# Two of VectorE's and TensorE's steps of an S5 scan given to GpSimd, in a fused decoder block

## What is computed

```python
lam_bar = jnp.exp(lam * dt)                       # complex, per state
b_bar = ((lam_bar - 1.0) / lam)[..., None] * bmat
bu = jnp.einsum("gpc,blgc->blgp", b_bar, ug.astype(jnp.complex64))
_, states = lax.associative_scan(_lin_rec, (a_el, bu), axis=1)   # s_t = lam_bar * s_(t-1) + bu_t
y = jnp.einsum("gcp,blgp->blgc", cmat, states).real + d_skip * ug
...
h = h + merged @ w_out[i]
```

## Time and profile before

| | |
|---|---|
| median of 3 runs | 1686.86 us (1686.63 to 1687.17) |
| the profiled execution, its time | 1687.59 us |
| its span from first to last instruction | 1686.0 us |
| granted TensorE clock, share of full speed | 0.998 |
| busy: PE, DVE, ACT, POOL | 1673.8, 1321.9, 971.6, 177.0 us |
| share of the span | 99%, 78%, 58%, 10% |
| DMA, mean | 209 GB/s |

### The profile page before, as it was taken

One profiled execution on the slowest core, in us unless ns is written; L12 is line 12 of the kernel. 1 busy time (PEld: TensorE's weight loads), 2 busy tenths in 40 slices (PEclk: granted clock), 3 DMA queues, 4 the chain that ended last, 5 costly groups with the idle time before them and its releaser, 6 DMA issues.

```text
span 1686.0 us, 24685 instructions
## 1 busy us (share of the span) xinstructions
PE 1673.8 (99%) x8468; PEld 1399.1 (83%) x8468; DVE 1321.9 (78%) x1677; ACT 971.6 (58%) x1271; POOL 177.0 (10%) x262
## 2 busy tenths in 40 slices
PE   9999999999999999999999999999999999999997
PEld 8888888888888888888878888888888888888886
DVE  7999999999998987545765868888888888845555
ACT  7776777667666667434547755444444444454553
POOL 7834201110000000000000200000000000000001
PEclk9999999999999999999999999999999999999999
DMA  7655555554566566666786577777777777756653
GB/s 254 213 185 175 185 173 179 169 181 163 196 218 219 190 220 187 201 197 195 243 266 208 170 231 243 241 241 244 243 243 242 236 245 236 234 190 198 190 188 123
DMA packets 167656, 352.19 MB, mean 209 GB/s; under 512 B 16112, under 2 KB 32672, under 8 KB 167456
## 3 DMA queue, kind: packets, MB, share of 16 engines
q1 hardware_dynamic: 162528, 338.26, 61.9%
q0 software_dynamic: 4336, 12.07, 2.1%
q10 hardware_dynamic: 720, 0.93, 0.2%
HBM read 335.41 MB, written 15.80 MB: 208 GB/s over the span
## 4 chain that ended last, share of the span: by engine, by line
PE 98%; DVE 1%; DMA 1%; SPq 0%; issue 0%; ACT 0%; DVEq 0%; POOL 0%; ACTq 0%; POOLq 0%
PE psum L1792 22%; PE psum L1794 22%; PE psum L1793 22%; PE psum L1753 19%; PE psum L1755 9%; PE psum L1842 1%; PE psum L1878 1%; PE psum L1832 1%; DMA merged_blocks<-flat_m 0%; PE psum L1804 0%; PE psum L1903 0%; PE psum L1879 0%; PE psum L1799 0%; DVE vn L1719 0%; PE psum L1809 0%; DMA quad_m<-merged_blocks 0%
## 5 line engine op out<-in xcount | busy, mean ns | idle before, releaser
L1085 DVE TENSOR_TENSOR wlo<-raw,whi 128x1024 fp32r<-128x1024 f32 x580 | 707.7, 1226 | 319.6 <-ACT whi L646 312.8
L646 ACT ACTIVATE whi<-raw 128x1024 fp32r<-128x1024 f32 x580 | 611.3, 1058 | 576.1 <-PE psum L1794 449.4
L1753 PE MATMUL psum<-act,whi 128*128 128x512 f32 x1088 | 342.6, 396 | 0.0
L1792 PE MATMUL psum<-whi,nw 128*128 128x512 f32 x704 | 274.1, 389 | 0.0
L1794 PE MATMUL psum<-whi,nw 128*128 128x512 f32 x704 | 273.9, 389 | 0.0
L1793 PE MATMUL psum<-wlo,nw 128*128 128x512 f32 x704 | 273.9, 389 | 0.0
L1755 PEld LDWEIGHTS psum<-act,wlo 128*128 128x128 f32 x1088 | 204.4, 188 | 48.3
L1755 PE MATMUL psum<-act,wlo 128*128 128x256 f32 x1088 | 213.8, 278 | 0.0
L1753 PEld LDWEIGHTS psum<-act,whi 128*128 128x128 f32 x1088 | 165.6, 189 | 3.3 <-issue 2.8
L1792 PEld LDWEIGHTS psum<-whi,nw 128*128 128x128 f32 x704 | 132.2, 188 | 27.5
L1794 PEld LDWEIGHTS psum<-whi,nw 128*128 128x128 f32 x704 | 132.2, 188 | 27.3
(11 more groups left out here) (249 smaller groups left out, 2283.9 us busy)
## 6 DMA issues: line engine op xcount, KB each, us to landing
raw<-in_w_up SPq DMA_DIRECT2D x176, 512.0 KB, 4.9
raw<-in_w_zx SPq DMA_DIRECT2D x96, 512.0 KB, 3.5
raw<-in_w_down SPq DMA_DIRECT2D x88, 512.0 KB, 3.8
raw<-in_w_gate SPq DMA_DIRECT2D x64, 512.0 KB, 5.1
raw<-in_w_proj SPq DMA_DIRECT2D x48, 512.0 KB, 4.4
raw<-in_w_bc SPq DMA_DIRECT2D x32, 512.0 KB, 3.5
raw<-in_w_glu SPq DMA_DIRECT2D x32, 512.0 KB, 4.4
raw<-in_w_out SPq DMA_DIRECT2D x32, 512.0 KB, 4.5
```

Of the source, the lines that this page charges most:

```text
L646: fn(whi[:, s, :], raw[:, s, :], ACTF.Copy).then_inc(hi_ready, 1)
L1085: V.tensor_tensor(wlo[:, s, :], raw[:, s, :], whi[:, s, :], ALU.subtract).then_inc(lo_ready, 1)
L1753: mm(psum[:, b + t, :], whi[:, s, cols(t)], x, start=first, stop=False)
L1792: mm(banks[:, t, :], x_hi, high[:, k], start=j == 0 and k == 0, stop=False)
```

## The change

1. **Inputs of the scans on GpSimd.** The subtraction `sx = rot[0] - rot[1]` leaves VectorE (`s5_inputs` is gone) and becomes `input_sum` on GpSimd. The scans wait for it (`input_ready`). On VectorE the sum of the group before now stands behind the turn back.
2. **Turned-on states added on GpSimd.** New is `state_sum`: GpSimd adds the second half of `st[r]` to the first, in place.
3. **Half of the output products.** TensorE then multiplies two terms for each tile and no longer four: 8 matmuls a block. It waits for GpSimd's addition (`state_ready`), no longer for VectorE's product (`x5_ready`).
4. **GpSimd's other work is spread.** The folds come one by one, two or three to a block, each behind the additions of a tile, and the dt chain comes in blocks 2 and 3. The loop over the later blocks is written out.
5. **Tables ahead of high part 0** on ScalarE.
6. **The load of `h` waits** for the last fetch of a merged chunk too (`m_read`, 128).

```diff
--- before.py
+++ after.py
...
@@ -545,8 +545,16 @@
                                   .rearrange("p c r n -> p r c n")).then_inc(cz_ready, 1)
                     pool.wait_ge(cz_ready, blk * 2 + (g + 1))
 
+            def input_sum(blk, r):
+
+                pool.wait_ge(bu_used, blk * 4 + (r + 1))
+                G.tensor_tensor(sx[:, :, :], rot[:, 0, :, :], rot[:, 1, ::-1, :], ALU.subtract
+                                ).then_inc(input_ready, 1)
+
+            input_sum(0, 0)
             pool.wait_ge(c_in, 16)
             fold(0)
+            input_sum(0, 1)
             fill_c(0)
             pool.wait_ge(u_ready, 4)
 
@@ -561,43 +569,75 @@
                 pool.wait_ge(y5_ready, i + 1)
                 fill_c(i + 1)
 
-            load_next(0)
-            fold(1)
+            def state_sum(blk, r):
+
+                pool.wait_ge(x5_ready, blk * 4 + (r + 1))
+                G.tensor_tensor(st[r][:, 0, :, :], st[r][:, 0, :, :], st[r][:, 1, ::-1, :], ALU.add
+                                ).then_inc(state_ready, 1)
+
+            def tile_sums(blk, *between):
+
+                for r in range(3):
+                    state_sum(blk, r)
+                    if blk or r:
+                        input_sum(blk, r + 1)
+                    if r < len(between):
+                        between[r]()
+
             dt = rs[0:DT, 0:P]
             ratio, square, series = (dtw[0:DT, k, :] for k in range(3))
-            pool.wait_ge(dt_inv, 1)
-            pool.wait_ge(vlo_ready, 1)
-            mul(ratio, dtd[0:DT, :], dte[0:DT, :])
-            mul(square, ratio, ratio)
-            step.done(G.tensor_scalar(series, square, 1.0 / 13, None, ALU.mult))
+
             def horner_steps(ks):
                 for k in ks:
                     step.done(G.tensor_scalar(series, series, 1.0 / k, None, ALU.add))
                     mul(series, series, square)
 
-            horner_steps((11, 9))
-            fill_next(0)
-            load_next(1)
-            fold(2, 2)
-            horner_steps((7, 5, 3))
-            step.done(G.tensor_scalar(series, series, 1.0, 2.0, ALU.add, ALU.mult))
-            mul(series, series, ratio)
-            step.done(G.tensor_scalar(square, dtx[0:DT, :], 0.0, None, ALU.max))
-            mul(dt, series, square, ALU.add)
-            G.tensor_scalar(ratio, dt, dtp[0:DT, 2:3], -1.0, ALU.mult, ALU.mult).then_inc(dt_row, 1)
-            pool.wait_ge(dt_row, 1)
-            for k, at_k in ((0, 0), (1, P), (1, L)):
-                pool.dma_start(scr[:, at_k:at_k + P], dtw[64 * k:64 * k + HEADS, 0, :]).then_inc(scr_w, 16)
-            fill_next(1)
-            load_next(2)
-            fold(4, 4)
-            fill_next(2)
-            with pool.Fori(3, 7) as i:
-                load_next(i)
-                fill_next(i)
-            pool.wait_ge(rot_free, 1)
+            def dt_first():
+
+                pool.wait_ge(dt_inv, 1)
+                pool.wait_ge(vlo_ready, 1)
+                mul(ratio, dtd[0:DT, :], dte[0:DT, :])
+                mul(square, ratio, ratio)
+                step.done(G.tensor_scalar(series, square, 1.0 / 13, None, ALU.mult))
+                horner_steps((11, 9))
+
+            def dt_second():
+
+                horner_steps((7, 5, 3))
+
+            def dt_third():
+
+                step.done(G.tensor_scalar(series, series, 1.0, 2.0, ALU.add, ALU.mult))
+                mul(series, series, ratio)
+                step.done(G.tensor_scalar(square, dtx[0:DT, :], 0.0, None, ALU.max))
+                mul(dt, series, square, ALU.add)
+                G.tensor_scalar(ratio, dt, dtp[0:DT, 2:3], -1.0, ALU.mult, ALU.mult).then_inc(dt_row, 1)
+                pool.wait_ge(dt_row, 1)
+                for k, at_k in ((0, 0), (1, P), (1, L)):
+                    pool.dma_start(scr[:, at_k:at_k + P], dtw[64 * k:64 * k + HEADS, 0, :]).then_inc(scr_w, 16)
+
+            def block_start(blk):
+
+                state_sum(blk - 1, 3)
+                input_sum(blk, 0)
+                fill_next(blk - 1)
+                if blk < 7:
+                    load_next(blk)
+
+            tile_sums(0, lambda: load_next(0), lambda: fold(1), lambda: fold(2))
+            block_start(1)
+            tile_sums(1, lambda: fold(3), lambda: fold(4), lambda: fold(5))
+            block_start(2)
+            tile_sums(2, lambda: fold(6), lambda: fold(7), dt_first)
+            block_start(3)
+            tile_sums(3, dt_second, dt_third)
+            for blk in range(4, 8):
+                block_start(blk)
+                tile_sums(blk)
+            pool.wait_ge(input_ready, 32)
             pool.wait_ge(scr_w, 48)
             load_decay(0, 0)
+            state_sum(7, 3)
             pool.wait_ge(y5_ready, 8)
             load_decay(0, 1)
             with pool.Fori(0, GROUPS - 1) as i:
@@ -606,6 +646,7 @@
                     load_decay(i + 1, half)
 
             pool.wait_ge(unit_used, UNIT0["out"])
+            pool.wait_ge(m_read, 128)
             pool.dma_start(h[:, :, :], a["x"]).then_inc(h_in, 16)
             nc.gpsimd.memset(cpad4[:, :, :], 0.0).then_inc(cpad4_ready, 1)
             pool.wait_ge(unit_used, UNIT0["out"] + 4)
@@ -784,10 +825,10 @@
                     before = (name, i, r - 1) if r else prev
                     last = name == "bc" and i == 1 and r == per - 1
                     group_hsum(*before)
-                    hi(0)
                     if r >= 2 or not start:
                         act.wait_ge(x5_ready, blk * 4 + (r - 1))
                     sines(r % 2, blk * 4 + (r + 1))
+                    hi(0)
                     hi(1)
                     group_tap(*before)
                     if not last:
@@ -1237,20 +1278,9 @@
                 V.tensor_tensor(rot[:, :, :, :].rearrange("p k c n -> p k (c n)"), twice(BU[r]), pairs(tab[r % 2][:, :, :]),
                                 ALU.mult).then_inc(bu_used, 1)
 
-            def s5_inputs(count, last):
-
-                dve.wait_ge(bu_used, count)
-                ins = V.tensor_tensor(sx[:, :, :], rot[:, 0, :, :], rot[:, 1, ::-1, :], ALU.subtract)
-                if last:
-                    ins.then_inc(rot_free, 1)
-                else:
-                    step.begun(ins)
-
-            def s5_scan(tile, last):
-
-                if last:
-                    dve.wait_ge(rot_free, 1)
-                step.hold()
+            def s5_scan(tile):
+
+                dve.wait_ge(input_ready, tile + 1)
                 m = s5k[:, 1, ds(tile, 1)].to_broadcast([P, L])
                 for k in range(2):
                     step.begun(V.tensor_tensor_scan(sx[:, k, :], m, sx[:, k, :], 0.0, ALU.mult, ALU.add))
@@ -1329,17 +1359,16 @@
                     last = name == "bc" and i == 1 and r == per - 1
                     tile = blk * 4 + r
                     lo(0)
+                    s5_turn_back(r, blk * 4 + (r + 1), blk, start and r == 0)
                     if r or start:
                         group_sums(*before)
-                    s5_turn_back(r, blk * 4 + (r + 1), blk, start and r == 0)
-                    s5_inputs(blk * 4 + (r + 1), last)
                     lo(1)
                     if last:
                         lo(2)
                     if r == 0 and not start:
                         s5_out(blk - 1, YS5)
                     group_conv(*before)
-                    s5_scan(tile, last)
+                    s5_scan(tile)
                     if not last:
                         lo(2)
                     cpad_free(*before)
@@ -1355,7 +1384,7 @@
             dve.wait_ge(parm_rest, 16)
             mixer_turn("zx", 0, 0, ("u", 0, 2))
             with dve.Fori(1, 6) as i:
-                step.enter(i, 4 * 3 + 2 * 5, 1)
+                step.enter(i, 4 * 2 + 2 * 5, 1)
                 mixer_turn("zx", i, i, ("zx", i - 1, 3))
                 step.leave(6)
             mixer_turn("bc", 0, 6, ("zx", 5, 3))
@@ -1835,12 +1864,11 @@
             def s5_products(blk, to):
 
                 pe.wait_ge(cz_ready, blk * 2 + 2)
-                pe.wait_ge(x5_ready, blk * 4 + 4)
-
-                for k in range(4):
+                pe.wait_ge(state_ready, blk * 4 + 4)
+
+                for k in range(2):
                     for r in range(4):
-                        ins = mm(to[32 * r:32 * r + 32], cz[:, r, (0, 1, 1, 0)[k], :], st[r][:, k // 2, k % 2, :],
-                                 start=k == 0, stop=k == 3)
+                        ins = mm(to[32 * r:32 * r + 32], cz[:, r, k, :], st[r][:, 0, k, :], start=k == 0, stop=k == 1)
                 ins.then_inc(y5_ready, 1)
 
             def mixer_turn(name, i, blk, prev):
```

More of the change, by code:

```diff
@@ L239, in build_program @@
             sem, ("s5_square", "s5_inv", "s5p_ready", "u_ready", "iota_ready", "angm_ready"))
-        ubs_ready, rot_free, bu_used, modulus_ready = map(
-            sem, ("ubs_ready", "rot_free", "bu_used", "modulus_ready"))
+        ubs_ready, bu_used, modulus_ready, state_ready, input_ready = map(
```

(1 more changed line is left out.)

## The result

Before 1687.01 us median (1686.63 to 1688.87, 4 runs), after 1722.43 (1720.26 to 1723.28, 4 runs): ratio 1.0205, 95% interval 1.0193 to 1.0218. The change makes the kernel 35 us **slower**; the forecast was 1719, the range 1690 to 1738. The profiled execution took 1722.47 us, its span is 1720.9.

The account below looks back on a forecast made before the run. TensorE, busy 99%, bounds the kernel before; VectorE was to set S5's pace after: 18.6 (zx) + 14.7 (bc) + 3.3 (folds) - 3 (lag) = +33.6 us, less 1.7 for the load, giving 1719 us, range 1690 to 1738.

Parts of the forecast that it names:

- The hole: VectorE in each S5 turn idles 1.28 us until ScalarE, behind its tables, makes the first high part; 5.1 us a block.
- 3.3 for the folds: Folds and dt chain beside the early zx blocks add 1.1 us of VectorE in each of three blocks.
- The input: GpSimd's subtraction holds a low part 0.70 us, or the first turn's convolution 0.75; its leaving saves VectorE 0.71 a turn.
- The state's addition: GpSimd's addition holds a low part 1.1 us, hidden in VectorE's idle time; only fourth turns pay, 0.65 us on the fractions.
- The blocks: VectorE sets S5's pace: zx blocks 50.8 us against 47.7, 18.6 us for six; bc turns 13.55 us each, 14.7 us more.
- GpSimd's own queue: Additions and loads of b on GpSimd fit into a turn: taken as 0, at most 0.5 us a block.
- the ring's lag: The ring of four units absorbs 4.9 us once, less 1.7 us of products waiting for the last state: 3 us off.
- The residual's load: In the out stage the later load of h removes TensorE's wait for act: 1.7 us less, at worst 0.
- The products: Eight of 16 output products a block go: TensorE saves 0.93 us a block, 7.4 us in all, if VectorE keeps up.
- Ahead: Rival: VectorE stays ahead in S5, its idle time costs nothing, TensorE's saving counts: 1678 us; chance 0.11.
- Beside each other: Rival: GpSimd's additions hold VectorE no more than the short ones did: 1687 us; chance 0.09.
- longer held: Rival: additions hold VectorE for 1.74 us less 0.15, 0.45 us more for each input: 24 us more, 1743; chance 0.06.

Follow-up runs that it names:

- tables_only: The kernel before with only ScalarE's tables moved ahead of the turn's first high part: 1717.40 us, ratio 1.0174.
- input_alone: The changed kernel without the state's addition (half the state missing from the output) and with the first high part ahead of the tables again: 1681.46 us, ratio 0.9960.
- no_state: The changed kernel with GpSimd's state addition left out, so half of the state is missing from the output: 1716.44 us, ratio 1.0175.
- tables_back: The changed kernel with only the tables' move undone, the first high part again ahead of them: 1694.59 us, ratio 1.0042.
- state_untimed: The changed kernel with the scans' input back on VectorE and the first high part ahead of the tables again: 1684.17 us, ratio 0.9972.
- both_timed: The changed kernel, high part ahead of tables again, state additions of each block's first three turns waiting for the second low part behind the fractions: 1688.97 us.
- h_only: The kernel before with only the load of h waiting for the last merged fetch: 1685.63 us, ratio 0.9983.

## Why the prediction was right, step by step

**The hole** was sized nearly right and is the loss. Forecast 1.28 us a turn; measured mostly 1.13 to 1.19 us idle (0.86 to 1.09 in some turns of the early blocks, and 2.36 in the first). The count without any hold (15 us in the zx blocks and 14.2 in the bc blocks, less 4.9 for the lag, as expected for tables_only, and the forecast's 3.3 for the folds) is 27.6 us; tables_only gave 30.

**The input.** Low part behind the group's sum 1.93 us instead of 1.22, forecast +0.70; the first turn's convolution 3.31 instead of 2.45, forecast +0.75. With what leaves VectorE the balance was to be nothing, and input_alone shows that.

**The state's addition** was to be hidden in the hole except for 0.65 us in each fourth turn, 5.2 us in all. no_state gave 6.0 back, but that the two are close is in part luck. The fractions took 0.70 more in only four turns. In the other three GpSimd, still busy when the states were ready, came behind the fractions and ran its addition in the hole, and TensorE waited 2.29 to 2.71 us for it; those blocks are only 0.1 us each longer than no_state's. Over half of the 6.0 lies in and behind the last block. This is the step of which the trace of before showed no like, and the reason behind it was only half right. I had GpSimd wait for VectorE's instruction in hand and then hold the next. By tables_back and state_untimed it often loses that boundary and waits through one or two low parts. In the changed kernel this made little difference: whichever goes first, the hole behind takes it up. At 396.50 the addition lost and ran in the hole; in a turn where it got in (293.06, 1.68 us) the two low parts took 3.57 us and no idle time was left between them.

**The blocks.** The six zx blocks were to cost 21.9 us with the folds; measured from first to seventh drive 308.43 us against 287.28: 21.2. By block it is less even: the fifth and sixth take 2.8 us more than before, where 3.1 were forecast, and the first four together 4.5 more than four such, where 3.3 were put down for the folds. A bc turn was to be 13.55 us and was 13.54. GpSimd's own queue was put at 0 to 0.5 us a block, which fits the 0.1 us just named; without the hole over it, it is in those early blocks that tables_back and both_timed lose.

**The step that failed** is the 3 us taken off for the ring's lag. The bc blocks up to the last product grew by 15.0 us (113.10 from 368.67, against 98.13 from 347.39), so all of the forecast 14.7 and none of the 3. The 3 were 4.9 us of lag less 1.7 for the last product's wait. That wait is there, 2.12 us:

```profile
481.77 1.07 PE L1871 MATMUL psum<-st,cz 128*32 128x256 f32 x16 [2.12 <-POOL st L575]
```

Without it the bc blocks grew by 12.85 us, 1.85 under the 14.7, so at most 1.85 of the 4.9 us of lag were had there. TensorE already waited for VectorE in the zx blocks (47.9 us busy of 50.5), so a lead was used up before the bc blocks; how much of it, no run shows. S5 is 36.2 us longer where the sum had 33.6, and that is most of the forecast's error of 3.4 us.

**The residual's load**: 1.7 forecast, 2.6 by h_only; in the changed kernel TensorE's wait for act is gone. The rest of the span, counted from the start of the last product, is only 1.3 us shorter, though that product itself takes 0.86 less: the stretch at the lower clock behind it takes some of it back. TensorE's timeline there, first and last:

```profile
482.77 0.50 PE L1821 MATMUL psum<-whi,act 128*128 128x512 f32 x1
...
486.46 0.45 PE L1821 MATMUL psum<-whi,act 128*128 128x512 f32 x1
```

Nine matmuls from start to start are 3.69 us, where nine just ahead of the wait, 0.227 us apart, would be 2.04: an estimate of 1.6 us. The prediction had no term for the clock.

**The products.** The forecast priced TensorE's saving at 0.93 us a block; it is 0.86, and it plays no part in the sum, because VectorE sets the pace.

**The rivals.** *Ahead* (1678) is what the change would be without the hole and without holds, and input_alone comes within 3.5 us of it. It was to need additions of under 1.1 us a turn; tables_back has no hole and lands at 1694.6, with two of its six zx blocks at Ahead's 46.86 us and VectorE busy in all of both. *Beside each other* fell with the low parts of 1.93 us, *longer held* with the same rows: 0.70 us of hold behind the group's sum, where it wanted 1.15.

By the Trainium skill (SBUF — State Buffer, Who interferes with whom) whoever comes first keeps the other out for the length of the instruction. Here GpSimd's 1.27 to 1.30 us cost VectorE up to 1.10, and rot, with an operand in PSUM, was never held (1.20 to 1.23 us in every run): the traces agree. Who goes first when one is waiting and the other issues back to back, the runs show both ways.

What **stays open**: what decides it. The same two additions, as far into the same instruction, took 1.68 and 3.94 us; a high part made just in time went with some of the early ones, but not with all, and no run was made that isolates it. Nor is it shown by a run of its own that the folds in GpSimd's queue are what makes the early blocks of tables_back and both_timed slow.

## What to carry to other kernels

When an instruction is moved ahead of another on a helper engine, ask what it waits for, and who waits for what now stands behind it: one high part behind tables that need the end of the last turn cost 30 us, more than everything else in this change put together. Run the parts of such a change alone: half of the products gains 3.5 us and the later load 2.6, and one unneeded move hid both. Where VectorE is full, try GpSimd's work beside instructions that read PSUM: it was worth 5.6 us with both additions on GpSimd, and nothing that could be measured with one. Two in a row on its queue reach the next instruction again, and an addition that TensorE needs should not stand behind other work on that queue.

## What the runs showed of the hardware

A GpSimd addition that meets VectorE's 128x512 or 128x1024 instructions with both operands in SBUF doesn't always get the next boundary: it took 3.87 to 3.96 us, through two low parts, in 20 of 32 cases of state_untimed, while the low parts kept their 2.35 us for two. I had expected it to cost VectorE 1.1 us each time. An addition that waits so costs VectorE nothing and makes its reader wait; one that gets in costs VectorE up to 1.10 us.
